# Mixture-of-experts loop on one core: two experts at a time, one in each half of the array's columns

## The reference, cut to what matters

```python
logits = x @ router_w + router_b
top_logit, top_e = lax.top_k(logits, 4)              # 4 of 32 experts for each token
gate = softmax(top_logit)
# for each expert e, over the tokens that chose it:
h = xb @ w_gu[e] + b_gu[e]                           # 1024 -> 2 x 1024
hg, hu = split(h);  hg = min(hg, 7);  hu = clip(hu, -7, 7)
act = (hu + 1) * hg * sigmoid(1.702 * hg)
y[token] += gate * (act @ w_down[e] + b_down[e])     # 1024 -> 1024
```

## Time and profile before

| | us |
|---|---|
| median of 3 runs | 1518.7 |
| lowest and highest | 1517.59, 1520.22 |
| the profiled execution, its own time | 1518.12 |
| its span, first to last instruction | 1516.1 |
| TensorE busy | 1442.1 (95% of the span) |
| VectorE busy | 527.7 (35%) |
| ScalarE busy | 283.3 (19%) |
| mean granted TensorE clock | 0.969 of 2.4 GHz |
| moved by DMA | 471.61 MB, mean 311 GB/s |

### The profile page before, as it was taken

How to read it: one execution, slowest core, us unless ns; L and a number is a source line. 1 busy time by engine, 2 the same in 40 slices (tenths; PEclk the granted TensorE clock), 3 DMA queues, 4 the chain that set the end, 5 groups by cost and what they waited for, 6 DMA issues and landing times.

```text
span 1516.1 us, 23691 instructions
## 1 busy us (share of the span) xinstructions
PE 1442.1 (95%) x9315; PEld 693.3 (46%) x9315; DVE 527.7 (35%) x1133; ACT 283.3 (19%) x493; POOL 106.9 (7%) x174
## 2 busy tenths in 40 slices
PE   6978899999999979999999999999999999999995
PEld 4755568866665633333333333333333333333332
DVE  6877665533312232232232222223223222222323
ACT  3111332211314022111111111111111111111111
POOL 1189600000000000000000000000000000000000
PEclk9998899997999989999999999999999999999997
DMA  7853111011667449999999999999999999999981
GB/s 313 181 128 55 55 62 58 31 57 58 271 249 316 192 182 385 428 428 428 428 429 428 428 429 428 428 429 428 429 429 428 429 428 428 428 429 429 429 380 43
DMA packets 42630, 471.61 MB, mean 311 GB/s; under 512 B 4880, under 2 KB 10128, under 8 KB 11088
## 3 DMA queue, kind: packets, MB, share of 16 engines
q1 hardware_dynamic: 36576, 461.42, 72.9%
q10 hardware_dynamic: 6000, 9.41, 3.3%
HBM read 465.07 MB, written 5.74 MB: 311 GB/s over the span
## 4 chain that ended last, share of the span: by engine, by line
PE 89%; DVE 5%; issue 3%; ACT 1%; DMA 1%; DVEq 0%; ACTq 0%; SPq 0%
PE bank L1027 29%; PE bank L1060 15%; PE bank L586 10%; PE bank L975 6%; PE bank L1085 5%; PE bank L669 2%; PE bank L839 2%; PE bank L990 2%; PE bank L982 2%; PE bank L1047 1%; PE bank L763 1%; PE bank L1038 1%; PE bank L755 1%; PE bank L730 1%; PE bank L738 1%
## 5 line engine op out<-in xcount | busy, mean ns | idle before, releaser
L1027 PE MATMUL bank<-big 128*64 128x512 f32 x2048 | 446.5, 594 | 0.7 <-ACT big L1323 0.7
L1027 PEld LDWEIGHTS bank<-big 128*64 128x64 f32 x2048 | 144.2, 137 | 288.6 <-issue 287.7
L1060 PE MATMUL bank<-big 128*64 128x512 f32 x1024 | 226.8, 595 | 0.2 <-ACT big L1337 0.2
L1874 DVE TENSOR_TENSOR big<-big,bank 128x320 f32<-128x320 f32 x256 | 104.9, 480 | 348.9 <-PE bank L1085 348.9
L586 PE MATMUL bank<-big 128*128 128x320 f32 (+1 forms) x688 | 189.0, 432 | 2.3 <-ACT big L1266 1.3
L586 PEld LDWEIGHTS bank<-big 128*128 128x128 f32 x688 | 131.4, 193 | 58.4 <-issue 7.8
L1060 PEld LDWEIGHTS bank<-big 128*64 128x64 f32 x1024 | 70.7, 137 | 132.1 <-issue 127.9
L1859 DVE TENSOR_SCALAR big<-bank 128x512 f32<-128x512 f32 x32 | 22.2, 693 | 310.0 <-PE bank L1027 310.0
L1332 ACT ACTIVATE big<-big 128x512 f32<-128x512 f32 x32 | 20.2, 632 | 486.0 <-DVE big L1859 486.0
L1119 ACT ACTIVATE big<-bank 128x320 f32<-128x320 f32 (+3 forms) x122 | 53.2, 436 | 263.1 <-PE bank L586 58.0
L975 PE MATMUL bank<-big 128*64 128x512 f32 x396 | 94.5, 613 | 0.0
(11 more groups left out here) (367 smaller groups left out, 1240.9 us busy)
## 6 DMA issues: line engine op xcount, KB each, us to landing
big<-in_w_gu SPq DMA_DIRECT2D x128, 2048.0 KB, 13.4
big<-in_w_down SPq DMA_DIRECT2D x64, 2048.0 KB, 12.9
big<-in_dense SPq DMA_DIRECT2D x47, 1024.0 KB, 8.0
big<-u_windows ACTq DMA_DIRECT2D x32, 160.0 KB, 7.2
out_y<-big SPq DMA_DIRECT2D x3, 512.0 KB, 2.7
big<-in_smw SPq DMA_DIRECT2D x1, 1408.0 KB, 19.4
big<-in_xT SPq DMA_DIRECT2D x2, 640.0 KB, 4.6
big<-in_consts SPq DMA_DIRECT2D x1, 1028.5 KB, 14.6
```

What stands on the lines that cost most here:

```text
L1027: last = mm(ps[bank][part, :], xte[:, k, :], w[:, at:at + 512], start=False, stop=(k == KT - 1))
L1060: last = mm(ps[4][part, :], actT[:, k % 4, (k // 4) * CAP:(k // 4 + 1) * CAP], w[:, k % 4, s * 512:s * 512 + 512], start=(k == 0), stop=(k ...
L1874: tt(part, part, ps[bank][:, 0:T], add).then_inc(psum_free[bank], 1)
```

## The change

Two experts are worked on together, 2n and 2n + 1; the loop has NP = 16 turns. The left half of the array's columns (ranks 0 to 63) belongs to the first expert, the right half to the second, so that all 128 PSUM partitions hold ranks of the pair.
- Up: each of four banks takes 512 of the 2048 columns; the two products side by side have different weights as well as different tokens. Down: two banks of 512 columns, in the same way.
- Gather, bias, scatter: one selection matrix of 128 columns for both experts, full-width products; the bias has four products of 32 rows, one for each bank; the scatter has eight products of 128 ranks. The weighted selection is transposed once per pair; the transposes of rows and activations are eight each per pair.
- The ring keeps its size and now holds half a pair's weights: loads alternate between the two experts, and the second half (loads 6 to 11) follows within the same turn, each two when a quarter of the up stage has used its two (`second_half`).
- PSUM banks are dealt out anew (`PAIR_USES`, `USE`, `SUM_BANK`), the rank and weight table is laid out per pair (`tab4`), several buffers move and grow, and the bias table is loaded in four DMAs instead of two. VectorE makes `selg` from `sel` by one multiplication.
- In the first turn `down_bias` stands in front of each of the eight scatter products, one bank at a time.

The diff, cut to its core:

```diff
-EXPERT_CHUNKS = 12
-LOADS = EXPERT_CHUNKS // 2
+NP = NE // 2
+LOADS = SLOTS // 2
...
+            def second_half(it, e):
+                for n in range(LOADS, 2 * LOADS):
+                    if n % 2 == 0:
+                        sp.wait_ge(S("load_used"), it * 4 + (n - LOADS) // 2 + 1)
+                    load(n, e)
...
+            for r in range(4):
+                sp.dma_start(BIG[32 * r:32 * r + 32, BIAS:BIAS + 512], a["b_gu"][0:NE, r * 512:r * 512 + 512]).then_inc(S("bias_in"), 16)
+            second_half(0, 0)
+            def load_pair(it, e):
+                for n in range(LOADS):
+                    if n == 0:
+                        sp.wait_ge(psum_full[3], nth(3, "up", it, 1))
+                    elif n == 2:
+                        sp.wait_ge(S("load_used"), it * 4)
+                    elif n == 4:
+                        sp.wait_ge(psum_full[4], nth(4, "down", it, 1))
+                    load(n, e)
+                second_half(it, e)
...
             def gather():
                 for t in range(TT):
-                    for s, part in sides:
-                        last = mm(ps[2][part, :], sel[:, t, :], htok[:, t, s * 512:s * 512 + 512], start=(t == 0), stop=(t == TT - 1))
+                    for h in range(2):
+                        last = mm(ps[5 + h][:, :], sel[:, t, :], htok[:, t, h * 512:h * 512 + 512], start=(t == 0), stop=(t == TT - 1))
...
             def start_bias():
-                for bank in (0, 1):
-                    row = slice(32 * bank, 32 * bank + 32)
-                    for s, part in sides:
-                        mm(ps[bank][part, :], biasrow[row, :], bias[row, s * 512:s * 512 + 512], start=True, stop=False)
+                for n in range(4):
+                    row = slice(32 * n, 32 * n + 32)
+                    mm(ps[n][:, :], biasrow[row, :], bias[row, :], start=True, stop=False)
...
+                for j in range(4):
+                    w = [view(loaded(2 * j + s, it), 2, 2 * FF) for s in range(2)]
+                    order = [(k, n) for k in range(2) for n in range(4)] if j < 3 else [(0, 0), (0, 2), (1, 0), (1, 2), (0, 1), (0, 3), (1, 1), (1, 3)]
+                    for k, n in order:
+                        for s, part in sides:
+                            last = mm(ps[n][part, :], xte[:, 2 * j + k, part], w[s][:, k, n * 512:n * 512 + 512], start=False, stop=end)
+                    if j < 3:
                         last.then_inc(S("load_used"), 1)
...
+                for n, bank in enumerate(SUM_BANK):
...
                     if first:
-                        for s in range(2):
-                            down_bias(4 * s + i, ps[banks[s]])
-                    for s, part in sides:
-                        mm(ps[banks[s]][:, 0:T], yb[part, i * P:(i + 1) * P], gtt[part, :],
-                           start=not first, stop=True).then_inc(psum_full[banks[s]], 1)
+                        down_bias(n, ps[bank])
+                    mm(ps[bank][:, 0:T], yb[:, n * P:(n + 1) * P], gtt, start=not first, stop=True).then_inc(psum_full[bank], 1)
...
-            step(ts(tabt[:, 0:TT, 0:NE], eg, -1.0, None, add))
-            step(tt(sel, over(con("iota")[:, 0:CAP], 1, TT), over(tab[:, 0, 0:TT], 2, CAP), ALU.is_equal), "selected")
-            step(cp(cur[:, 0:TT], tab[:, 0, 0:TT]))
+            for t in range(TT):
+                step(ts(tabt[:, 0, t, 0:NP], eg[:, t].rearrange("p (n s) -> p n s", s=2), -1.0, None, add))
+            step(cp(ranks, tab[:, 0, 0:6]))
+            step(tt(sel6, iota, over(ranks, 2, CAP), ALU.is_equal), "selected")
...
+                for h in range(2):
+                    dve.wait_ge(psum_full[h], nth(h, "up", it))
+                    ts(hg, ps[h][:, :], LIMIT, None, ALU.min).then_inc(psum_free[h], 1)
+                    dve.wait_ge(psum_full[2 + h], nth(2 + h, "up", it))
+                    ts(hu, ps[2 + h][:, :], LIMIT, -LIMIT, ALU.min, ALU.max).then_inc(psum_free[2 + h], 1)
```

More of the change, by code:

```diff
@@ L436, in all_passes @@
                 first()
-            with eng.Fori(1 if first else 0, NE) as e:
+            with eng.Fori(1 if first else 0, NP) as e:
                 expert(e, e)
@@ L473, in build, with nth, ahead @@
         gate4 = view(SIG, TT, P)
-        SCATTER_BANKS = ((6, 7), (3, 5), (4, 2), (6, 7))
+        PAIR_USES = {0: (0, 1), 1: (0, 1), 2: (0, 1), 3: (0, 1), 4: (1, 5), 5: (1, 4), 6: (2, 4), 7: (0, 4)}
+        AHEAD = {(5, "gather"): 1, (4, "rows"): 1, (6, "gather"): 1, (6, "rows"): 2}
+        USE = {0: ("up",), 1: ("up",), 2: ("up",), 3: ("up",), 4: ("gates", "rows", "down", "sum3", "sum7"),
+               5: ("gather", "act", "sum0", "sum4"), 6: ("gather", "rows", "sum1", "sum5"), 7: ("act", "down", "sum2", "sum6")}
+        SUM_BANK = (5, 6, 7, 4, 5, 6, 7, 4)
+        def nth(bank, use, it, back=0):
+            ahead, each = PAIR_USES[bank]
+            return it * each + (BANK_USES[bank] + ahead + USE[bank].index(use) + 1 - back * each)
+        def ahead(bank, use):
+            return BANK_USES[bank] + AHEAD[bank, use]
         block = ctx.enter_context(nc.Block())
@@ new lines, in activations @@
+                def activations(h, bank):
+                    pe.wait_ge(S("activated"), it * 2 + (h + 1))
+                    for i in range(4):
+                        last = nc.tensor.transpose(ps[bank][:, i * P:(i + 1) * P], columns[:, h, i], ident)
+                    last.then_inc(psum_full[bank], 1)
+                if first:
+                    stored(pe, "gt")
+                else:
+                    pe.wait_ge(psum_free[7], nth(7, "sum6", it, 1))
+                activations(0, 7)
@@ new lines, in expert @@
+                pe.wait_ge(psum_free[4], nth(4, "gates", it))
+                pe.wait_ge(psum_free[5], nth(5, "gather", it))
+                gathered(0)
+                activations(1, 5)
+                pe.wait_ge(psum_free[6], nth(6, "gather", it))
+                gathered(1)
+                pe.wait_ge(psum_free[7], nth(7, "act", it))
+                pe.wait_ge(psum_free[4], nth(4, "rows", it))
+                for d in range(2):
+                    w = [view(loaded(8 + 2 * d + s, it), 4, D) for s in range(2)]
+                    order = [(i, h) for i in range(4) for h in range(2)] if d == 0 else [(i, h) for h in range(2) for i in range(4)]
+                    if d:
+                        pe.wait_ge(psum_free[5], nth(5, "act", it))
+                    for i, h in order:
+                        end, bank = (d, i) == (1, 3), (7, 4)[h]
+                        for s, part in sides:
+                            last = mm(ps[bank][part, :], actT[:, 4 * d + i, part], w[s][:, i, h * 512:h * 512 + 512], start=(d == 0 and i == 0), stop=end)
+                        if end:
+                            last.then_inc(psum_full[bank], 1)
+                    if d == 0:
@@ L1328, in _ @@
+            for h in range(2):
+                copy_xte(h, ahead((4, 6)[h], "rows"))
             copy(gateT, "gt")
             def expert(it, e):
[L1331 to L1335 removed]
@@ L1342, in _ @@
+                copy_act(0, 7)
+                copy_xte(0, nth(4, "rows", it))
+                copy_act(1, 5)
+                copy_xte(1, nth(6, "rows", it))
+                for h, bank in enumerate((7, 4)):
+                    act.wait_ge(psum_full[bank], nth(bank, "down", it))
+                    af(yb[:, h * 512:h * 512 + 512], ps[bank][:, :], ACT.Identity).then_inc(psum_free[bank], 1)
             all_passes(act, expert)
```

276 lines of the change are left out of this document (124 added, 152 removed).

## The result

The kernel after takes 1525.58 us (median of 5 runs, 1524.52 to 1526.26) against 1518.7: a ratio of 1.0049, interval 1.0037 to 1.006. The forecast was 1524.5 us, slower than before.

A forecast was written before the change was run, and what follows sets the result against it. Weight transfers were taken to bound the new loop, 58.7 us a pair against TensorE's 56.2. Late first load, lost DMA and last pair put the last addition at 1499.2; with the unchanged norm, span 1522.0, forecast 1524.5 us, range 1518.5 to 1532.

The forecast's parts named there:

- The backlog of before as a hidden second bound: Expert loop before: six loads take 29.37 us, TensorE 0.2 us less per expert; saving beyond that turns into waiting for weights.
- the signs of being right: Up stage near 557.5, landing time flat after the fourth pair, waits 2.5 us, period 58.7, last addition near 1499.
- TensorE's work of a pair: Loop: TensorE's stages for two experts sum to 56.2 us, 2.1 less than before; loads take 58.7.
- The start: Ahead of the loop: wider selection and a half-clock first gather make the up stage begin at 557.5, 3.5 us late.
- First load: First pair's up stage: load 7 issued at 564.4, 6.6 us later than before, landing at 573.4.
- The dry queue in the first pair: First pair's scatter: interleaved down bias takes 11.8 us instead of 5.9, so 4.0 us of DMA is lost once.
- The tail: Behind the loop: final norm from last addition to the span's end stays the same, 22.8 us.
- The sum: End of the loop: last landing 1482.9, last addition 1499.2 against 1493.3; span 1522.0, +5.9.
- The rival of the clock: Loop waits lower TensorE's clock; the last pair's loss adds 1.7 us, 1526, up to 1530; chance 0.15.
- The cheap start: Start and first pair: up begins at 556, down bias keeps 5.9, no DMA lost; +0.4, about 1519; chance 0.2.
- the room in the loads: Loop: 428 GB/s is only TensorE's demand, so a pair takes 56.2 us; some 1485; chance 0.05.
- TensorE as the bound: Loop: bias products one by one and copies uncovered make 60.1 us a pair, over 58.7; 1540 or more; chance 0.06.

The follow-up runs named there:

- light_after: Kernel after, every weight transfer except the first six bringing half its bytes, that part of the weights left out: 1469.14 us, one timing.
- bias_batched: Kernel after with the first pair's down bias in two groups of four 32-row products together, each ahead of four scatter products: ratio 1.0033 to the kernel before.
- light_before: Kernel before, every weight transfer except the first six bringing half its bytes, that part of the weights left out: 1516.72 us, one timing.
- pe_pad: Kernel after with two more full 512-column products (1.72 us) ahead of every pair's gather: ratio 1.0078 to the kernel before.
- warm_after: Kernel after with twelve idle TensorE products while VectorE picks the experts, meant to keep the clock up for the first gather: ratio 1.0056 to the kernel before.
- combined: Kernel after with batched first-pair down bias, loads 6 and 7 of each pair fetched in halves, and twelve idle products: ratio 1.0019 to the kernel before.
- two_dmas: Kernel after with every 2 MB weight transfer issued as two of 1 MB back to back: 1538.75 us, ratio 1.0138 to the kernel before.
- warm_before: Kernel before with twelve idle TensorE products while VectorE picks the experts: ratio 0.9986.
- warm_bias_before: Kernel before with twelve idle products and the first expert's down bias in two groups of four 32-row products: 1513.18 us, ratio 0.9962.
- both warm2 kernels: Kernel after with twelve plus three idle products ahead of the loop, without and with batched first-pair down bias: ratios 1.006 and 1.0047 to the kernel before.
- warm2_after: Kernel after with twelve idle products during expert selection and three more between rank counts and first gather: ratio 1.006 to the kernel before.

## Why the prediction was right, by its steps

- *The backlog of before as a hidden second bound.* Right, and it decides the case: 58.74 us a pair was forecast as 58.7, and light_after shows that nothing but the transfers holds the new loop. Time to landing stayed at 15.3 to 15.4 us from 710 to 1454 us, as the signs of being right had it.
- *TensorE's work of a pair.* 56.2 forecast, 54.63 measured. The term that was off most is the transposes, 2.88 against 1.99; gather 5.44 against 5.17 and down 14.04 against 13.89 are the next. It changed nothing in the sum, since the transfers bound it, only the wait: 3.7 instead of 2.5, in two places instead of one. The bias (1.02, measured 1.07) and the scatter (4.6, measured 4.5) were right.
- *The start.* 3.5 us late was forecast; from the rank product to the up stage it is 13.83 against 10.13, 3.7. The clock came back at 552.3 against 551.1 in the kernel before, as much later as the rank product.
- *First load.* 7.8, not 9.0, from issue to landing; the up stage's first quarter was 7.1 with the issue.
- *The dry queue in the first pair.* 4.0 forecast, about 3.3 by bias_batched (above). The issue at 628.3 landed at 636.0, as forecast (628.4, 636.1), and the interleaved bias took 0.74 a step, though the first pair as a whole was shorter than forecast (62.3 for 64.0). bias_batched saved 4.8 us of TensorE's work there (from the first up stage's begin to SP's first down load issued behind that scatter are 71.6 us, 560.73 to 632.34, for 76.4, 558.81 to 635.21). Over the whole loop the transfers lost more than was taken: from the first load's landing (573.7) to the last (1484.2) are 910.5 us, and 185 loads of 4.895 are 905.6, so 4.9 were lost where 4.0 had been put down.
- *The tail.* Taken as unchanged, 22.8; it is 24.4. This is the term that the prediction had wrong, put at nothing although the change adds two products behind the loop: they take 2.0 us (1504.58 to 1506.59), of which 0.4 is made up because TensorE starts sooner after the last addition. The tail also varies without any edit behind the loop: 22.8 in the kernel before, 20.2 in light_before.
- *The sum.* The last addition ends at 1499.4, forecast 1499.2, and that this is so close is in part luck: the up stage begins 1.3 late (1.1 of it from before any changed instruction), the transfers lose 0.9 more, and what follows the last wait takes 34.6 us for 35.9 since TensorE's work was taken too high.
- *The rival of the clock.* It was there: a granted clock under 1 in the loop, which the prediction had named as a sign of being wrong, stands in 7 of the 14 pairs from the third on. Windows of two pairs of the kernel after, and the restart in the second of them, from the timeline:

```profile
1149.65:1208.38 58.73, 55.04 (x249) 21.75 (x247) 10.97 (x20) 7.22 (x12) 0.00 (x0) 1.00 1.01 429
738.54:797.27 58.73, 56.53 (x249) 22.34 (x247) 10.96 (x21) 7.22 (x12) 0.00 (x0) 0.97 1.01 428
...
759.92 8.78 PE L1066 MATMUL bank<-big 128*64 128x512 f32 x32 [2.20 <-DMA big<-in_w_gu]
```

The clock of 0.97 costs TensorE 1.5 us of work in the second, in the quarter that follows a wait of 2.2 us (8.78 us for the usual 7.09), and the waits are shorter by that; both pairs take 58.7. In the last pair of this run it stayed at full speed, so it cost nothing. That is chance: in pe_pad, warm_after, combined and two_dmas it fell in the last pair, whose last quarter then took 8.7 to 8.8 us instead of 7.1. So the rival's price of 1.7 was right, and it is paid in some executions. The Trainium skill ("TensorE: Matmul & The Clock Gate", section "HAM oscillation — how this bites in real kernels") tells of a loop that falls back to half clock in each turn; its waits for DMA are some 3 to 5 us. The prediction took that as speaking for a fall in every pair here, where the waits are shorter: with 2.2 to 2.8 us it is so in half of the pairs.
- *The cheap start and the room in the loads* are refuted by the start (3.7) and by light_after together with the 4.895 us a load. *TensorE as the bound* is refuted by pe_pad.

Open: why the time from TensorE's last instruction in the loop to its first behind it is 5 to 13 us. It goes with the packets of 16 KB that the instruction queue q8 moves in that time: one where it is 5.05 (light_before, warm_before, warm_bias_before, and there VectorE's release ends it), two where it is 5.7 to 7.0 (the kernel before, the kernel after and seven more), five where it is 13.0 to 13.4 (both warm2 kernels). Queue q8 in that stretch of light_before, the kernel before and warm2_after:

```profile
q8 instruction: 1, 0.02, 1.2%
...
q8 instruction: 2, 0.03, 2.1%
...
q8 instruction: 5, 0.08, 3.5%
```

This fits a TensorE that waits for its own instructions, but no run changed only that, and the profile does not say for which engine a packet is.

## What to carry to other kernels

When two resources both look busy all the time, compare the time to landing of the same transfer early and late in the loop: if it grows, the transfers are the slower ones, and work saved on the engine will turn into waits. A ring that is refilled by whole stages delays the first refill by a whole stage; where the transfers set the end, the time of the first refill and every dry stretch are paid in full. What is worth trying in such a kernel is outside the loop: here some 3.3 us of 1518 in the clock and the first expert's bias. And what a change adds behind a loop (two products, 1.6 us) is part of its sum.

## What the runs showed of the hardware that was not expected

- The same bytes in smaller transfers cost the backlogged queue more time: 2 MB in one transfer, in packets of 16 KB, took 4.895 us, in two of 1 MB, in packets of 8 KB, 4.97 (59.63 / 12).
- Two pauses of TensorE of 1.2 and 1.4 us, with small products between, were followed by half clock (warm_after, from 547 us), while with the second pause filled (warm2_after) the clock stayed at 1.00, and waits of 2.8 us in the loop were followed by half clock in only some pairs.
- The first instruction of TensorE behind the long loop came 7.0 us after the last one in the loop in the kernel before (1491.86 to 1498.87), 5.7 in the kernel after, 5.05 in warm_bias_before and 13.4 in warm2_after. The end of warm2_after moved by 7 us with it, in four of its six timings by their length; fifteen more products ahead of the loop are all that its program has over the kernel after.
